# A two-layer hybrid transformer block on one core: first modulation pair loaded first, rotary turns moved to ScalarE, and three queues reordered

## The chip, the cores and the metric

The kernel runs on one core of a Trainium2 chip. The metric is the device time of the program in microseconds. TensorE does the matrix products, VectorE, ScalarE and GpSimd (POOL in the profile) the elementwise work, and SyncE (SP) issues all the transfers from HBM.

## The reference, cut to what matters

Two layers are applied to 256 tokens x and, beside them, 256 context tokens, all of width 1024 in float32. The second layer's context output is not needed.

```python
for l in range(DEPTH):                       # DEPTH = 2
    m  = silu(c) @ w_mod[l] + b_mod[l]       # six shifts, scales and gates for x
    mc = silu(c_ctx) @ w_mod[l] + b_mod[l]   # and for the context
    h, hc = rmsnorm(x)*g*(1+sc1)+sh1, rmsnorm(xc)*g*(1+csc1)+csh1
    a_b, a_c, a_u, q, k, v, r_g, r_u, d_v, d_g, gl = split(h @ w_in)
    y_b = window_attention(rotate(q), rotate(k), v, k_ctx, v_ctx, sink)
    ys = (short_conv(...) @ w_a_out, y_b @ w_b_out,
          (gelu(r_g) * rglru_bidir(...)) @ w_c_out,
          silu(layernorm(dwconv31(...))) @ w_d_out)
    x = x + gt1 * (sum(sigmoid(gl) * ys) @ w_out)
    x = x + gt2 * swiglu(rmsnorm(x)*g2*(1+sc2)+sh2)
out = rmsnorm(x) * g_final
```

In rotate, the 128 dimensions of a head are four blocks of 32: t becomes t*cos + (-t2, t1, -t4, t3)*sin. In the kernel the sign is part of the sine table, so that the turned operand is t with its blocks swapped in pairs.

## The kernel before

Activations are stored transposed: the 1024 features are eight rows (k = 0 to 7) of 128 partitions, the tokens are columns. W is 512 columns in layer 0 (tokens and context) and 256 in most stages of layer 1. Every float32 product is made from three products in a rounded format: the high part HH (or ZH) of the activation, its low part HL (ZL), and the high and low parts WH and WL of the weights. ScalarE makes a high half by a copy (`high`), POOL or VectorE makes the low half by a subtraction (`low`).

Weights come in slabs of 1 MB, two output tiles of 128 columns over all eight rows. There are two slots, s = 0 and 1, for RAW, WH and WL. A slab passes these steps: SP's load when both low halves of the slab before it in this slot are made, two high halves of 1024 columns on ScalarE, two low halves on POOL (in some stages of layer 1 the second on VectorE), 48 products on TensorE (line 474), then evacuation on ScalarE and VectorE. Slab n+2 is made ready by ScalarE and POOL while TensorE works at slab n+1. Two slabs are a pair; a stage is 4 to 8 slabs. The order of the work on each engine is written out by hand. Every engine works in its own order and waits for semaphores.

**Start.** SP loads x, then slab 0, then the eight modulation slabs of layer 0's first norm as four pairs (L383). TensorE sums squares, and then for each pair: 16 small products in 32 records (`mod_rows_of`, L579), a product that turns the rows to columns (`mod_columns`), and the products of the two rows of the pair before (`first_rows`). ScalarE copies the rows (`mod_copy`) and makes HH, VectorE makes MOD, AMP, S and HL.

**Keys and queries.** After the slabs of kv and q, ScalarE copies a tile to SBUF, TensorE multiplies it by the permutation ROT into bank 6 or 7 (`rotate`), and VectorE adds the cosine part and the turned sine part (`cosines`, `turned`). There is one such turn for the keys and one for each of the four query slabs, in each layer. With the last q slab come the first scores of attention, for head 0. The first d_in slab is cut up by the parts of head 0's attention; in layer 0 its scores of a third unit (the context's queries) come after 12 products and wait for query slab 2.

**a_out.** In the third pair of a_out (slabs 4 and 5) the layer norm of the conformer branch is finished: eight rows, for each one product with the norm's gain on VectorE, a sigmoid on ScalarE and a gate on VectorE. VectorE's `stage(..., some=(2, 3))`, which takes slabs 4 and 5 out of the banks, comes after it.

**Second norm.** After w_out, `norm_root` and `norm` prepare the rows of the feed-forward input. ScalarE's order is: roots and diagonals, `high` of slab 1 of ff_in0, a table load for the sigmoid, then the rows' HH (`norm_high`). POOL makes the low part of every second of the later rows (`norm_low`), behind both low halves of slab 1.

Of the kernel before, what the change touches and what calls it, by code (L numbers as in the profile page):

```python
# [22 lines left out]
DEPTH = 2  # L23
D = 1024
KC = D // P
# [115 lines left out]
def build(nc, stream, modw, lruw, xT, cT, prm, rope, consts, outT):  # L141
    with ExitStack() as ctx:
# [124 lines left out]
        def stage_sems(l):  # L267
# [39 lines left out]
            st("kv_a", "c0 v0 x0 x1")  # L307
            st("kv_v", "a0 a1 b0 s0 b1 s1")
            st("kv_p", "r0 r1")
            st("q_a", "c0 c1 x0 x1" if l == 0 else "c0 c1")  # L310
            st("q_v", "a0 b0 s0 b1 s1")
            st("q_p", "r0 r1")
# [53 lines left out]
        def _(sp):  # L366
# [63 lines left out]
        def _(pool):  # L430
# [27 lines left out]

            for first, end, halves in [r for r in runs if r[2]]:
                for l in range(DEPTH):  # L460
                    if first == pair_base(l, "ff_in0") + 1:
                        norm_low(l, "n2", seqs_of(l))
                    if l > 0 and first == pair_base(l, "kv") + 1:
                        norm_low(l, "n1", 2)
                with pool.Fori(first, end) as m:
                    for s in range(2):
                        for h in range(halves):
                            low(m, s, h)


        @block.tensor
        def _(pe):
# [201 lines left out]
            for p in range(MOD_FIRST // 2):  # L674
                pe.wait_ge(first_loaded[p], 32)
                for s in range(2):
                    mod_rows_of(s, MOD_HOMES[2 * p + s], p, s, 2)
                if p > 0:
                    pe.wait_ge(L[0]["mod_v"].sem, L[0]["mod_v"].at(0, f"m1_{p - 1}"))
                mod_columns(p, 2, PS[:, 4, 0:4 * MOD_FIRST].rearrange("p (h x) -> p h x", h=2)[:, :, 4 * p:4 * p + 4])  # L680
                if p > 0:
                    first_rows(2 * p - 2)
                    first_rows(2 * p - 1)
            first_rows(KC - 2)
            first_rows(KC - 1)
            for l in range(DEPTH):
# [26 lines left out]
                def rotate(st_a, st_p, n, s):  # L713
                    for t in range(2):
                        if f"c{t}" in st_a.names:
                            pe.wait_ge(st_a.sem, st_a.at(n, f"c{t}"))
                        else:
                            out_of(pe, l, "kv", 0)
                        mm(bank(6 + s, NX, t * NX), ROT, KR[t][:, 0:NX] if st_a is a["kv_a"] else QR[s][t], True, True).then_inc(st_p.sem, 1)


# [14 lines left out]
                pe.wait_ge(a["ci_a"].sem, a["ci_a"].at(KC - 1, "i1"))  # L736
                rotate(a["kv_a"], a["kv_p"], 0, 0)
# [35 lines left out]
                for n in range(1, 4):  # L773
# [1284 lines left out]
```

## Time and profile before

| | us |
|---|---|
| time, median of 3 runs | 2063.46 (2060.65 to 2063.71) |
| the profiled execution | 2059.77 |
| its span | 2058.0 |
| TensorE busy | 2025.8 (98%) |
| VectorE busy | 1110.7 (54%) |
| ScalarE busy | 880.6 (43%) |
| POOL busy | 820.2 (40%) |

The span goes from the first to the last instruction on the chip; what lies around it, 1.8 us here, is launch and end. Matmul records overlap, since their ends are modelled: the step from one start to the next is what a product costs. A float32 product without the three-part form has two records.

### The profile page before, as it was taken

The page shows a single profiled execution, that of the slowest core. Times are in us where ns is not written, and L with a number is a line of the kernel's source. Part 1 is how long each engine was busy: PE and PEld are TensorE (multiplying, and loading weights), DVE is VectorE, ACT ScalarE, POOL GpSimd, SP SyncE. Part 2 cuts the span into 40 slices and gives each one's busy share as a digit, 9 for nine tenths or more (in the row PEclk, how much of TensorE's full clock was granted, in tenths as well). Part 3 has the DMA queues.
Part 4 walks back from the last instruction along what each step waited for, and adds up shares of the span by engine and source line. Part 5 has one row for each costly group of instructions (what it writes and reads, how often), then busy time and mean ns, then how long its engine had stood idle before and what let it go on. Part 6 is the DMA issues. An engine that isn't in the chain of part 4 may idle for free.

```text
span 2058.0 us, 30588 instructions
## 1 busy us (share of the span) xinstructions
PE 2025.8 (98%) x11694; PEld 1695.7 (82%) x11694; DVE 1110.7 (54%) x2036; ACT 880.6 (43%) x1381; POOL 820.2 (40%) x355
## 2 busy tenths in 40 slices
PE   7999999999999999999999999999999999999998
PEld 4778788888888778777777788777899999999998
DVE  5895455567789741123111111479756888644555
ACT  4795444231222342224222212379765444545444
POOL 1003222343434444333334334410446887354443
PEclk9999999999999999999999999999999999999999
DMA  8222211222222223654534422422333555454553
GB/s 338 85 69 82 82 62 51 89 86 102 82 102 83 101 89 130 251 228 195 223 112 164 165 101 82 159 68 84 121 122 123 184 184 188 165 180 162 187 184 143
DMA packets 38705, 278.45 MB, mean 135 GB/s; under 512 B 4416, under 2 KB 4416, under 8 KB 5312
## 3 DMA queue, kind: packets, MB, share of 16 engines
q1 hardware_dynamic: 38592, 276.87, 37.1%
q8 instruction: 80, 1.31, 0.3%
q14 instruction: 33, 0.27, 0.0%
HBM read 275.80 MB, written 1.05 MB: 135 GB/s over the span
## 4 chain that ended last, share of the span: by engine, by line
PE 93%; DVE 2%; DMA 2%; ACT 2%; issue 1%; POOL 1%; SPq 0%; DVEq 0%; POOLq 0%; ACTq 0%
PE PS L474 90%; PE PS L579 2%; PE PS L756 1%; POOL WL L434 1%; DMA S<-in_modw 1%; ACT WH L852 1%; DMA RAW<-in_stream 1%; DMA CD<-in_lruw 0%; DVE PS L1301 0%; DVE CD L1304 0%; ACT TMP L852 0%; DVE LT L1304 0%; DVE HL L1304 0%; DVE WL L1301 0%; DVE X L1304 0%
## 5 line engine op out<-in xcount | busy, mean ns | idle before, releaser
L434 POOL TENSOR_TENSOR WL<-RAW,WH 128x1024 fp32r<-128x1024 f32 x336 | 808.9, 2426 | 1214.8 <-ACT WH L852 1214.8
L474 PE MATMUL PS<-HH,WH 128*128 128x512 f32 (+1 forms) x2272 | 800.0, 352 | 9.8 <-DVE HL L1304 4.9
L474 PE MATMUL PS<-HH,WL 128*128 128x512 f32 (+1 forms) x2272 | 778.9, 343 | 0.0
L474 PE MATMUL PS<-HL,WH 128*128 128x512 f32 (+1 forms) x2272 | 778.8, 343 | 0.0
L852 ACT ACTIVATE WH<-RAW 128x1024 fp32r<-128x1024 f32 x416 | 417.4, 1052 | 719.7 <-PE PS L474 666.1
L474 PEld LDWEIGHTS PS<-HH,WH 128*128 128x128 f32 x2272 | 429.3, 189 | 79.1 <-issue 22.5
L474 PEld LDWEIGHTS PS<-HL,WH 128*128 128x128 f32 x2272 | 429.7, 189 | 57.6 <-issue 5.5
L474 PEld LDWEIGHTS PS<-HH,WL 128*128 128x128 f32 x2272 | 429.0, 189 | 55.4
L474 PE MATMUL PS<-ZH,WH 128*128 128x512 f32 (+1 forms) x992 | 336.9, 340 | 2.8 <-POOL WL L434 1.7
L474 PE MATMUL PS<-ZH,WL 128*128 128x512 f32 (+1 forms) x992 | 335.6, 338 | 0.0
L474 PE MATMUL PS<-ZL,WH 128*128 128x512 f32 (+1 forms) x992 | 335.5, 338 | 0.0
L1304 DVE SCALAR_TENSOR_TENSOR PS<-G,PRM,PS 128x512 f32<-128x512 f32 (+1 forms) x464 | 254.3, 613 | 0.1
L474 PEld LDWEIGHTS PS<-ZH,WH 128*128 128x128 f32 x992 | 186.8, 188 | 29.0 <-issue 4.3
L474 PEld LDWEIGHTS PS<-ZH,WL 128*128 128x128 f32 x992 | 186.7, 188 | 22.7
L474 PEld LDWEIGHTS PS<-ZL,WH 128*128 128x128 f32 x992 | 186.8, 188 | 22.3
L1301 DVE TENSOR_TENSOR TMP<-TMP,PS 128x512 f32<-128x512 f32 (+1 forms) x56 | 31.6, 564 | 282.5 <-ACT TMP L852 267.9
L852 ACT ACTIVATE TMP<-PS 128x256 f32<-128x256 f32 (+1 forms) x173 | 84.2, 486 | 124.4 <-PE PS L756 52.1
L1301 DVE TENSOR_TENSOR PS<-TMP,PS 128x256 f32<-128x256 f32 (+1 forms) x84 | 46.2, 549 | 163.8 <-ACT TMP L852 149.5
L1301 DVE TENSOR_TENSOR WL<-RAW,WH 128x1024 fp32r<-128x1024 f32 x80 | 118.0, 1492 | 14.9 <-ACT WH L852 14.9
L1304 DVE SCALAR_TENSOR_TENSOR X<-PS,MOD,X 128x256 f32<-128x256 f32 (+1 forms) x96 | 41.3, 477 | 127.8 <-PE PS L474 127.7
L852 ACT ACT_TABLE_LOAD x50 | 64.2, 1283 | 1.6 <-PEq L2051 0.7
L474 PE MATMUL PS<-TMP,S 128*128 128x128 f32 (+2 forms) x288 | 61.4, 357 | 1.1 <-DVE CD L1301 1.1
(174 smaller groups left out, 1497.2 us busy)
## 6 DMA issues: line engine op xcount, KB each, us to landing
RAW<-in_stream SPq DMA_DIRECT2D x208, 1024.0 KB, 4.8
CD<-in_modw SPq DMA_DIRECT2D x42, 1024.0 KB, 7.1
CD<-in_lruw SPq DMA_DIRECT2D x2, 2048.0 KB, 8.3
X<-in_xT SPq DMA_DIRECT2D x2, 1024.0 KB, 8.1
S<-in_modw SPq DMA_DIRECT2D x2, 1024.0 KB, 14.0
G<-in_modw SPq DMA_DIRECT2D x2, 1024.0 KB, 22.0
RAW<-in_modw SPq DMA_DIRECT2D x1, 1024.0 KB, 17.0
TMP<-in_modw SPq DMA_DIRECT2D x1, 1024.0 KB, 18.8
```

The lines of the kernel that those rows point to most:

```text
L434: nc.gpsimd.tensor_tensor(WL[:, a:b], RAW[:, a:b], WH[:, a:b].bitcast(F32), ALU.subtract)\
L474: return nc.tensor.matmul(out, lhs, rhs, start=start, stop=stop)
L579: last = nc.tensor.matmul(PS[32 * g:32 * g + 32, 5 + q % 2, 0:2 * P], SILC[:, at:at + 32], w[:, k * 2 * P:(k + 1) * 2 * P], start=j == 0 a ...
L756: last = nc.tensor.transpose(bank(4 + u, P, q * P), PR[u % 2][:, q * P:(q + 1) * P], IDENT)
L852: return nc.scalar.activation(out, in_, f, **kw)
L1301: return V.tensor_tensor(out, x, y, op)
L1304: return V.scalar_tensor_tensor(out, x, sc, y, op0, op1)
```

## The change

It has five parts.

1. SP issues the first two modulation slabs ahead of weight slab 0, and the other six behind it. On TensorE, the pairs and the rows are woven: pair 0, columns 0, row 0, pair 1, row 1, columns 1, pair 2, row 2, columns 2, row 3, pair 3, row 4, columns 3, rows 5 to 7. ScalarE makes slab 0's high parts after the first `mod_copy`.
2. ROT's products are gone. ScalarE copies the four blocks of 32 partitions straight to their swapped places in bank 6 or 7, for both tiles at once, from the banks (queries) or from SBUF (keys). It waits until VectorE has read the bank's earlier contents. In layer 1, VectorE's cosines of a query tile wait for these copies. The first scores follow the last q slab.
3. In layer 1, slab 4 of a_out is gated and added before the layer-norm loop, its successor's first high half is made there too, the second high half after row 1, and the first of VectorE's low halves inside its loop.
4. ScalarE makes only the first high half of slab 1 of ff_in0 ahead of the second norm's rows, the second between or behind them, and loads the sigmoid table at the end.
5. POOL makes the low parts of those norm rows before the second low half of slab 1.

```diff
@@ sync
-            load(0, 0)
             for j, n in enumerate(MOD_ORDER):
+                if j == 2:
+                    load(0, 0)
@@ gpsimd
-                with pool.Fori(first, end) as m:
+                with pool.Fori(first, end - (end - 1 in ff_first)) as m:
...
+                if end - 1 in ff_first:
+                    l = ff_first.index(end - 1)
+                    for s, h in ((0, 0), (0, 1), (1, 0)):
+                        low(end - 1, s, h)
+                    norm_low(l, "n2", seqs_of(l))
+                    low(end - 1, 1, 1)
@@ tensor
+            first_mods(0)
+            first_columns(0)
+            first_rows(0)
+            first_mods(1)
+            first_rows(1)
+            first_columns(1)
+            first_mods(2)
+            first_rows(2)
+            first_columns(2)
+            first_rows(3)
+            first_mods(3)
+            first_rows(4)
+            first_columns(3)
+            for k in range(5, KC):
+                first_rows(k)
...
-                pe.wait_ge(a["ci_a"].sem, a["ci_a"].at(KC - 1, "i1"))
-                rotate(a["kv_a"], a["kv_p"], 0, 0)
...
-                    if n == 3:
-                        for u in range(2):
-                            scores(0, u, 0, 0)
-                        pe.wait_ge(a["q_v"].sem, a["q_v"].at(0, "s1"))
-                    rotate(a["q_a"], a["q_p"], n - 1, (n - 1) % 2)
-                pe.wait_ge(a["q_v"].sem, a["q_v"].at(1, "s1"))
-                rotate(a["q_a"], a["q_p"], 3, 1)
+                for u in range(2):
+                    scores(0, u, 0, 0)
@@ scalar
-            high(0, 0)
             for p in range(MOD_FIRST // 2):
                 mod_copy(p, p)
+                if p == 0:
+                    high(0, 0)
...
+                def swapped(source, s):
+                    for q in range(4):
+                        to, at = slice(32 * q, 32 * q + 32), slice(32 * (q ^ 1), 32 * (q ^ 1) + 32)
+                        last = fn(PS[to, 6 + s, 0:NT].rearrange("p (t n) -> p t n", t=2), source[at, :, 0:NX], ACT.Copy)
+                    return last
...
+                swapped(CD[:, 4 * NT:6 * NT].rearrange("p (t n) -> p t n", t=2), 0).then_inc(ks.sem, 1)
...
-                    for t in range(2):
-                        fn(QR[s][t], bank(2 * s + t, NX), ACT.Copy).then_inc(qs, 1)
+                    if n < 2:
+                        if s == 0:
+                            act.wait_ge(a["kv_v"].sem, a["kv_v"].at(0, "s1"))
+                    else:
+                        act.wait_ge(a["q_v"].sem, a["q_v"].at(n - 2, "s1"))
+                    swapped(PS[:, 2 * s:2 * s + 2, :], s).then_inc(qs, 1)
...
+                if l:
+                    tiles(b, 0)
+                    gate("ao")(4, 0, b)
+                    high(b + 1, 0, range(1))
...
+                    if l and k == 1:
+                        high(b + 1, 0, range(1, 2))
...
-                high(pair_base(l, "ff_in0"), 1)
+                high(pair_base(l, "ff_in0"), 1, range(1))
+                norm_high(l, "n2", 24, C, between=lambda: high(pair_base(l, "ff_in0"), 1, range(1, 2)))
                 table(ACT.Sigmoid)
-                norm_high(l, "n2", 24, C)
@@ vector
+                if l:
+                    dve.wait_ge(tile_done[0], 2 * (pair_base(l, "a_out") + 2) + 2)
+                    gated("ao")(4, 0, pair_base(l, "a_out") + 2)
...
+                    if l and k == 3:
+                        low(pair_base(l, "a_out") + 3, 0)
```

## Rows read from the trace of the kernel before

**Rows 1.** The page: busy time, share of the span, instructions.
```profile
PE 2025.8 (98%) x11694; PEld 1695.7 (82%) x11694; DVE 1110.7 (54%) x2036; ACT 880.6 (43%) x1381; POOL 820.2 (40%) x355
```
**Rows 2.** TensorE's waits: for whom, total us, times, longest.
```profile
PE PS L474 <- DVE HL L1304: 4.9, 5, 2.6
...
PE PS L474 <- DVE S L1301: 3.7, 1, 3.7
```
**Rows 3.** TensorE's timeline, start: start, us, what, count, idle before and its releaser.
```profile
19.36 3.57 PE L579 MATMUL PS<-S,SILC 128*32 128x256 f32 x32 [2.24 <-DMA S<-in_modw]
...
27.31 0.58 PE L474 MATMUL PS<-SELB,TMP 128*128 128x4 f32 x4 [1.12 <-ACT TMP L852]
...
46.31 0.50 PE L474 MATMUL PS<-HH,WH 128*128 128x512 f32 x1 [0.35 <-DMA CD<-in_lruw]
```
**Rows 4.** Timelines of VectorE, ScalarE and POOL, start.
```profile
17.87 3.35 DVE L1412 RECIPROCAL TMP<-TMP 128x512 f32<-128x512 f32 x1 [5.87 <-ACT TMP L852]
...
30.05 1.66 DVE L1304 SCALAR_TENSOR_TENSOR HL<-S,MOD,HH 128x256 fp32r<-128x256 f32 x4
...
42.51 1.99 ACT L852 ACTIVATE WH<-RAW 128x1024 fp32r<-128x1024 f32 x2
...
43.63 4.77 POOL L434 TENSOR_TENSOR WL<-RAW,WH 128x1024 fp32r<-128x1024 f32 x2 [20.08 <-ACT WH L852]
```
**Rows 5.** DMA issues of the first 60 us: count, KB each, median us to landing.
```profile
S<-in_modw SPq DMA_DIRECT2D x2, 1024.0 KB, 14.0
...
CD<-in_lruw SPq DMA_DIRECT2D x1, 2048.0 KB, 7.5
```
**Rows 6.** TensorE's timeline, layer 0, end of q and start of d_in.
```profile
222.75 1.88 PE L474 MATMUL PS<-TMP,S 128*128 128x512 f32 x4
224.46 1.89 PE L474 MATMUL PS<-S,CST 128*128 128x256 f32 x8
226.00 0.58 PE L474 MATMUL PS<-HH,WH 128*128 128x512 f32 x1
...
230.22 0.48 PE L474 MATMUL PS<-TMP,S 128*128 128x256 f32 x1 [1.07 <-DVE CD L1301]
```
**Rows 7.** Timelines of ScalarE, VectorE, POOL and TensorE, layer 1, kv and q.
```profile
1449.60 1.08 ACT L852 ACTIVATE CD<-PS 128x512 f32<-128x512 f32 x2 [0.73 <-PE PS L474]
...
1465.40 0.43 DVE L1301 TENSOR_TENSOR PS<-PS,ROPE 128x256 f32<-128x256 f32 x1 [0.64 <-PE PS L474]
...
1469.95 0.70 ACT L852 ACTIVATE TMP<-CD 128x256 f32<-128x256 f32 x2
...
1471.73 2.01 ACT L852 ACTIVATE WH<-RAW 128x1024 fp32r<-128x1024 f32 x2
...
1472.87 5.21 POOL L434 TENSOR_TENSOR WL<-RAW,WH 128x1024 fp32r<-128x1024 f32 x2 [1.40 <-ACT WH L852]
...
1479.03 0.42 ACT L852 ACTIVATE ZH<-TMP 128x256 fp32r<-128x256 f32 x1 [5.30 <-DVE TMP L1304]
...
1481.03 9.48 POOL L434 TENSOR_TENSOR WL<-RAW,WH 128x1024 fp32r<-128x1024 f32 x4 [2.94 <-ACT WH L852]
...
1493.48 0.47 PE L474 MATMUL PS<-HH,WH 128*128 128x256 f32 x1
```
**Rows 8.** Timelines of ScalarE and TensorE, layer 1, a_out.
```profile
1768.36 1.99 ACT L852 ACTIVATE WH<-RAW 128x1024 fp32r<-128x1024 f32 x2
...
1769.58 0.36 PE L474 MATMUL PS<-HH,WH 128*128 128x256 f32 x1 [3.74 <-DVE S L1301]
```
**Rows 9.** Timelines of TensorE and ScalarE at the second norms.
```profile
936.22 0.47 PE L474 MATMUL PS<-HH,WH 128*128 128x512 f32 x1 [1.54 <-DVE HL L1304]
...
1855.84 1.28 ACT L852 ACT_TABLE_LOAD   x1
...
1858.36 0.35 PE L474 MATMUL PS<-HH,WH 128*128 128x256 f32 x1 [2.60 <-DVE HL L1304]
```
**Rows 10.** Stretches: length, busy us of PE, PEld, DVE, ACT, POOL, then granted clock.
```profile
1770.00:1774.00 4.00, 4.00 (x23) 4.00 (x22) 3.71 (x4) 0.62 (x2) 2.81 (x1) 0.57 0.55 160
```

More of the change, by code:

```diff
@@ L672, in first_rows, with first_mods @@
                         last.then_inc(tile_done[0], 1)
-            for p in range(MOD_FIRST // 2):
+            def first_mods(p):
                 pe.wait_ge(first_loaded[p], 32)
@@ L711, in _ @@
                     gates(n - 1)
-                def rotate(st_a, st_p, n, s):
-                    for t in range(2):
[L715 to L719, printed above, removed]
                 b = pair_base(l, "kv")
@@ L852, in fn, with high @@
                 return nc.scalar.activation(out, in_, f, **kw)
-            def high(m, s):
+            def high(m, s, halves=range(2)):
                 act.wait_ge(raw_loaded[s], 16 * m + 16)
-                for h in range(2):
+                for h in halves:
                     x = slice(s * SLAB + h * HALF, s * SLAB + (h + 1) * HALF)
@@ L956, in diagonals, with norm_high @@
                     fn(tmp(1, c * P, (c + 1) * P), IDENT, ACT.Identity, scale=tmp(0, m + c, m + c + 1)).then_inc(inverse, 1)
-            def norm_high(l, nm, shift, c_all, some=None):
+            def norm_high(l, nm, shift, c_all, some=None, between=None):
                 na, nv = L[l][nm + "_a"].sem, L[l][nm + "_v"].sem
@@ L970, in norm_high @@
                         ins.then_inc(na, 1)
+                    if between is not None and k == (KC - 3 if c_all == 2 else KC - 1):
+                        between()
             def decay(l):
@@ L1230, in _ @@
                     fn(bank(5 + k % 2, W), row(CD, k, W), ACT.Sigmoid, bias=par(l, "ln_b", k)).then_inc(la.sem, 1)
-                    if k == KC // 2:
+                    if k == KC // 2 and l == 0:
                         tiles(b, 0)
                         high(b + 1, 0)
+                    if l and k == 1:
+                        high(b + 1, 0, range(1, 2))
                 table(ACT.Sigmoid)
-                gate("ao")(4, 0, b)
+                if l == 0:
+                    gate("ao")(4, 0, b)
                 tiles(b, 1)
@@ L1635, in _ @@
                     if n < 2:
-                        turned(a["q_v"], a["q_p"], n, n % 2, lambda t: query(n, t))
+                        turned(a["q_v"], a["q_a"], n, n % 2, lambda t: query(n, t))
                 dv, da = a["di_v"], a["di_a"]
@@ L1850, in _ @@
                         ln_gate(k - 1)
+                    if l and k == 3:
+                        low(pair_base(l, "a_out") + 3, 0)
                 ln_gate(KC - 1)
-                stage(l, "a_out", gated("ao"), some=(2, 3))
                 b = pair_base(l, "a_out") + 3
+                for s in range(l, 2):
+                    dve.wait_ge(tile_done[s], 2 * b)
+                    gated("ao")(4 + s, s, b - 1)
+                    if l:
+                        low(b, s)
                 dve.wait_ge(tile_done[0], 2 * b + 2)
```

31 lines of the change are left out of this document (11 added, 20 removed).

## The prediction

> **What bounds the kernel now.** I read the page first, then the waits of TensorE, then its timeline, and beside each of its gaps the timelines of the engine that ended the gap. The page says TensorE is busy 98% of a span of 2058.0 us [rows 1]. So only two things shorten the time: work taken off TensorE, and its gaps. The longest gaps stand in the waits [rows 2] and, one by one, in the timelines. Eight are longer than 0.9 us, and the change works at those of the modulation at the start [rows 3], of the first d_in slab of layer 0 [rows 6], the third a_out pair of layer 1 [rows 8], and the second norm of both layers [rows 9]. A gap can cost more than its length. After the 3.74 us gap at 1769.58 and the 2.60 us gap at 1858.36 the granted clock was at its lower level, 1.2 GHz, for a while (0.57 on the mean of 1770 to 1774) [rows 10]; after 1.07 us at 230.22 it stayed at 2.4 GHz. Counted in products, 24 of them took 4.44 us after the gap at 1769.58 and 2.85 us later: 1.6 us lost. I use 1.6 to 1.7 us for each such fall. The query slabs of layer 1 [rows 7] have no such gap yet. The Trainium skill (TensorE: Matmul & The Clock Gate, "What's actually happening") has the throttled state as the default and lets activity release it; by that rule a new gap is paid twice as well, and the trace agrees.
>
> **1. Rotary turns leave TensorE.** A call of rotate is two products, four records; two calls take 226.00 - 224.46 = 1.54 us [rows 6], 0.77 us a call. Five calls in each layer go. In their place ScalarE makes four copies of 32 partitions by 512. No row shows so few partitions. The nearest is the 128x512 copy: two in 1.08 us, a start every 0.50 [rows 7]. Below: if the price went by data moved, a quarter of that, 0.5 us for four; above: four that don't overlap at 0.60, 2.4 us. I take the whole price, 4 x 0.50 + 0.1 = 2.1 us, since the row's length goes with the columns. The Trainium skill (ScalarE: Activation LUTs, "What ACT_TABLE_LOAD costs") has one element a cycle in each lane, so that few partitions save nothing; by its figures four such copies are an estimated 2.1 us. No row here can show it.
>
> Layer 0, slabs of 11.3 us. The copies are hidden: the timelines have the weights of slab 2 ready at 195.1 and used at 199.2, and ScalarE's part comes 1.6 us later (without that slack of 4.1 us, 1.6 in each of two slabs). The turns of kv, q0 and q1 are saved: 3 x 0.77 = 2.3 us. Those of q2 and q3 are not. They stand between the scores (222.75) and the first d_in slab (226.00), which runs 12 products and then waits until 230.22 for VectorE [rows 6]. VectorE's chain begins with the scores, 7.5 us earlier, and its order is not changed. So the 1.54 us turn into a longer gap: 1.07 + 1.54 + about 0.2 = 2.8 us. It lies where the clock fell in the other rows (2.24, 2.60, 3.74) and above 1.54, where it did not: I count a fall at 7 in 10, +1.2. Term: -2.3 + 1.2 = **-1.1 us**.
>
> Layer 1, slabs of 5.7 us. Here the chain is short of time already: the last q slab waits 0.3 us in mid-slab for POOL (1485.85). ScalarE now copies kv's blocks after its last square roots: from 1469.95 [rows 7] to 1472.05. VectorE needs 1.7 us for its multiply and add (from 1465.40 [rows 7] to 1467.09 before, hidden then): 1473.8. The copy of q0 uses the same bank 6, so ScalarE waits for that, copies until 1475.9, and only then makes the high half of slab q2's weights, which is queued behind: 1475.85 where it was 1471.73 [rows 7], +4.1. POOL's first low half ends near 1475.5 before [rows 7], so 1479.6 after. TensorE would be there at 1477.27 - 2 x 0.77 = 1475.7: a gap of 3.9 us and a fall of the clock. Slab q2 ends at 1479.6 + 5.7 + 1.7 = 1487.0. Meanwhile VectorE takes q0's cosines 4.3 us later and with them its last two scans; ScalarE's ZH copy, which waits for these [rows 7], moves from 1479.03 to 1483.3. Behind it: copies of q1 until 1485.8, high half of slab q3 at 1485.7 (before 1479.88), POOL 1486.85 to 1489.25 and 1491.6 (two halves at 2.4) [rows 7]. Slab q3 starts at 1489.3 after a gap of 2.3 us, gets its second half at 1491.6, ends at 1495.9, or at 1496.9 with the clock down. With 1.7 us of scores d_in starts at 1497.6 or 1498.6; before 1493.48 [rows 7]. Term: +4.1 to +5.1, taken **+4.7 us**. With four copies at 0.5 us each chain link falls by 1.6: +0.5; at 2.4 us by 0.9: +5.6.
>
> **2. Start.** SP issues the first modulation pair ahead of the first weights. At some 420 GB/s a 1 MB slab lands every 2.5 us; the pair in S (14.0 us median from issue to landing) [rows 5] is there 2.5 us sooner, at 16.7 instead of 19.2. The weights land at 19.2, pair 2 at 24.2 as before. TensorE comes from the square sums at 17.0 with no gap and at the full clock, so pair 1 takes 1.9 us, as pairs 2 to 4 do, instead of 3.57 [rows 3], and ends near 19.0. That gains little: VectorE's reciprocal ends only at 17.87 + 3.35 = 21.22 [rows 4]. From there 0.5 for MOD and AMP, 1.7 for four S, 0.9 for the first two HL: row 0 at 24.3. ScalarE's weights (19.4 to 21.4) and POOL's low half (22.9) are in time. Then TensorE's order is rows 0, pair 2, row 1, columns 2, and so on. Rows 2 and 3 need columns + 2.74 + 0.85 = 3.6 us (27.31 to 30.05) [rows 3, 4], and the columns now stand behind a row. Without a low clock: row 0 to 25.7, pair 2 to 27.6, row 1 to 29.0, columns 29.0, row 2 at 32.6, columns 34.0, row 4 at 37.7, columns 39.1, rows 6 and 7 42.7 to 45.5. But between 19.0 and 24.3 TensorE has only the small column products, a gap in which I expect the clock to fall: +1.6 us ahead of the first columns, so last columns at 40.8. The next slab starts when ScalarE and POOL have made slab 1's weights, queued behind the last HH: HH ends 3.4 us after the columns, POOL's half 3.5 us after that (42.51 to 46.0) [rows 4]. So 47.7 against 46.31 [rows 3]; lruw lands 7.5 us after the last pair's products [rows 5], 47.1, and is not late. Ends: -0.3 (no fall) and +2.7. Term **+1.3 us**.
>
> **3. a_out, layer 1.** The gap of 3.74 us at 1769.58 is the wait for VectorE's gated sum of slab 4, which stands behind the whole layer-norm loop [rows 8]. Now gate and sum come ahead of it (done 1761.3), slab 6's first high half at 1760.4, its low half at 1764.0: slab 6 starts where slab 5 ends, 1765.6. That is 3.9 us earlier and no fall of the clock: 5.5 us. What is late next is slab 7. The loop starts 1.0 us later and now holds one low half of 1.2 us, ends at 1769.4; ScalarE's high half for slab 7 follows at 1769.0 (before 1768.36 [rows 8]), POOL's low half is done at 1772.7. TensorE is there at 1771.3: 1.4 us given back. Bounds -5.5 (slab 7 in time) and -2.5 (loop 1.6 us longer). Term **-4.2 us**.
>
> **4. Second norm.** ScalarE did two high halves (2.0) and a sigmoid table (1.3 + 0.2) ahead of the first HH [rows 9]; now one half. Layer 1: scaled rows are there at 1855.0, so HH 1855.05, HL 1855.5, first product 1856.1 instead of 1858.36 [rows 9]. Rows then come at VectorE's and POOL's pace: row 3 at 1859.05, row 7 at 1861.9, slab over at 1862.6 against 1865.7. The held-back half gives slab 1 its last low weights at 1864.5 where 1864.0 is wanted: 0.5. Term 3.1 - 0.5 = **-2.6 us** (bounds -3.5 and -1). Layer 0: four scaled rows end at 934.2, HL 935.1, so 1.0 us of the 1.54 at 936.22 [rows 9] goes; half 2 comes after row 5 and brings rows 6 and 7 back to their old times (POOL 944.1 and 945.4): **-0.7 us**.
>
> **Sum:** +1.3 - 1.1 + 4.7 - 4.2 - 2.6 - 0.7 = **-2.6 us**. Between these places TensorE runs without a gap, so that the terms add. The profiled execution took 2059.77 us (span 2058.0), so 2057.2 after; the median of the runs shown, 2063.46, is 3.7 us higher, and the forecast for the median is 2063.46 - 2.6 = **2060.9 us**. What counts as no change is 0.2%, 4.1 us, about what a measurement of this kernel can tell.
>
> **Rivals.** (a) The q chain of layer 1 holds: the copies cost by data, 0.5 us for four, or the wait for bank 6 costs little. Then that term is +0.5 and the sum -6.8: **2056.7**. For it: nothing but the small number of partitions. Against: every ScalarE row goes with its columns. (b) The other side: copies from PSUM to PSUM, of which no row shows any, take turns at reading and writing and cost double, 4.1 us for four. They are links of chains at three places. In layer 1 q0's and q1's copies stand one behind the other ahead of slab q3: 2 x 2.0 = +4.0. In both layers q3's copies stand ahead of the first exponential, which now leaves ScalarE idle until 2.5 us after the scores begin and would wait until 4.2: some +1.5 each. Sum -2.6 + 4.0 + 3.0 = +4.4: **2067.9**. For it: the copies read banks that VectorE's cosines read at the same time. Against: 256 columns cost 0.28 from PSUM to SBUF and no more where VectorE was reading too. It decides from where four cost 2.1 + 2.6/3.5 = 2.8 us: beyond that the kernel is slower than before. (c) The gaps close as planned and the clock never falls in the new ones: start -0.3, layer 0 -2.3, layer 1 +3.0, a_out -5.5, norms -4.0: -9.1, **2054.4**. For it: after 1.54 us at 936.22 the clock stayed up; against: two of the new gaps are well over 2 us.
>
> **Chances.** Forecast 0.60, of which 0.05 falls beyond 4.1 us on the fast side; (a) 0.18, (c) 0.10, (b) 0.12. So faster 0.33, same 0.55, slower 0.12. Range 2054.5 to 2066.0: it takes in (a), the bounds of the forecast's terms and half of what lies toward (b), and leaves out most of (c) and the far end of (b), under 2 in 10.
>
> **What would show it.** Start: first 512-column product near 24.3, second slab near 47.7. Layer 0: gap of 2.5 to 3 us before the third unit's scores. Layer 1: a new gap near 4 us before slab q2 that POOL ends, one near 2 us before q3, and four 32x512 copies at 0.5 us. a_out: no gap before slab 6, 1 to 2 us before slab 7. Second norm of layer 1: gap under 0.5 us and no low clock. Copies under 0.3 us each, or a q2 gap under 1 us, would make the prediction wrong.

## The result, and the profile after

| | before | after |
|---|---|---|
| median, 8 runs each, us | 2063.10 (2060.53 to 2063.71) | 2068.15 (2066.84 to 2069.74) |
| the profiled execution, us | 2059.77 | 2068.54 |
| its span, us | 2058.0 | 2066.8 |

The ratio is 1.0026, with an interval of 1.0018 to 1.0035: the kernel became slower by about 5.0 us. The forecast was 2060.9 us, 2.6 us faster than before, with a range of 2054.5 to 2066.0: both were wrong. The first fence shows the page of the profile after, the second its waits of TensorE (for whom, total us, times, longest); they answer to [rows 1, 2].

```profile
PE 2020.5 (98%) x11654; PEld 1690.7 (82%) x11654; DVE 1114.0 (54%) x2036; ACT 898.6 (43%) x1405; POOL 820.3 (40%) x355
```

```profile
PE PS L478 <- DVE HL L1328: 13.5, 7, 7.3
PE PS L478 <- POOL WL L433: 11.3, 9, 4.3
```

TensorE is busy 5.3 us less, with ten turns (40 records) gone, and its waits have grown by more. The wait for HL was 4.9 us with a longest of 2.6; it is now 13.5 us with one of 7.3. The wait for POOL's WL now holds one of 4.3 us. Both are in places where TensorE had none that long.

The timeline of TensorE after gives the places (start, us, what, count, idle before and its releaser):

```profile
17.54 1.94 PE L583 MATMUL PS<-S,SILC 128*32 128x256 f32 x32
...
27.90 0.80 PE L478 MATMUL PS<-HH,WH 128*128 128x512 f32 x1 [7.32 <-DVE HL L1328]
...
51.39 0.47 PE L478 MATMUL PS<-HH,WH 128*128 128x512 f32 x1 [0.17 <-issue]
...
232.71 0.80 PE L478 MATMUL PS<-TMP,S 128*128 128x256 f32 x1 [2.79 <-DVE CD L1325]
...
938.43 0.48 PE L478 MATMUL PS<-HH,WH 128*128 128x512 f32 x1 [1.33 <-DVE HL L1328]
...
960.58 0.64 PE L583 MATMUL PS<-CD,SILC 128*32 128x256 f32 x8 [1.38 <-DMA CD<-in_modw]
...
1484.12 0.36 PE L478 MATMUL PS<-HH,WH 128*128 128x256 f32 x1 [4.29 <-POOL WL L433]
...
1493.95 0.38 PE L478 MATMUL PS<-HH,WH 128*128 128x256 f32 x1 [1.95 <-POOL WL L433]
...
1511.45 0.38 PE L478 MATMUL PS<-TMP,S 128*128 128x128 f32 x1 [1.28 <-DVE CD L1325]
...
1785.34 0.39 PE L478 MATMUL PS<-ZH,WH 128*128 128x256 f32 x1 [1.25 <-POOL WL L433]
...
1864.74 0.36 PE L478 MATMUL PS<-HH,WH 128*128 128x256 f32 x1 [0.40 <-DVE HL L1328]
```

The 9984 products of the weight slabs come in the same order in both kernels. So the shift, the start of a product after less the start of the same product before, says where time is lost or won:

| stretch | shift at its end, us | change in it | predicted |
|---|---|---|---|
| start, to slab 1 | +5.1 | +5.1 | +1.3 |
| layer 0, q to the third unit's scores | +3.9 | -1.2 | -1.1 |
| layer 0, second norm and first modulation loads behind it | +4.2 | +0.3 | -0.7 |
| layer 1, up to the end of kv | +3.8 | -0.4 | 0 |
| layer 1, q and first d_in slab | +11.4 | +7.6 | +4.7 |
| layer 1, d_in to the middle of a_out | +12.6 | +1.2 | 0 |
| layer 1, third a_out pair | +8.6 | -4.0 | -4.2 |
| layer 1, second norm, to the end of slab 1 of ff_in0 | +6.2 | -2.4 | -2.6 |
| layer 1, the rest of the feed-forward, to the last product | +8.8 | +2.5 | 0 |

The profiled executions are 8.8 us apart and the medians 5.0. The two long stretches without an edit give +1.2 and +2.5 us. Most of that is a different rate of TensorE's products in the two executions, as the last section shows. Of the 2.5 us, 0.8 is a longer wait for POOL near the end (1.51 us where it was 0.63); over all kernels, those with nothing changed near it included, this wait was anywhere from 0.63 to 1.51 us. The -0.4 us of layer 1 up to kv is a fall of the clock ahead of layer 1's first norm, in the profile before and not in this one.

In layer 0's norm the shift falls by 1.7 us up to the slab at 938.43 and rises by 2.0 behind it, 1.38 of that at the wait at 960.58. The clock was low ahead of this slab in the profile before (0.57 from 931.00 to 934.60) and not in this one, but that isn't what brought the 1.7 us. rotary_only, which has the norm of before, ran here without a fall as well, and its slab started at the same place relative to the kernel before, behind a longer gap, 2.99 us for 1.54:

```profile
935.58 0.47 PE L472 MATMUL PS<-HH,WH 128*128 128x512 f32 x1 [2.99 <-DVE HL L1297]
```

**The start.** These are timelines of VectorE and POOL after, and then three groups by tile (count, ns shortest/median/longest, first and last start):

```profile
22.02 1.36 DVE L1328 SCALAR_TENSOR_TENSOR AMP<-MOD,PRM 128x2 f32<-128x2 f32 x2
23.41 3.64 DVE L1328 SCALAR_TENSOR_TENSOR S<-X,AMP,TMP 128x256 f32<-128x256 f32 x4
26.98 1.66 DVE L1328 SCALAR_TENSOR_TENSOR HL<-S,MOD,HH 128x256 fp32r<-128x256 f32 x4
...
20.95 4.64 POOL L433 TENSOR_TENSOR WL<-RAW,WH 128x1024 fp32r<-128x1024 f32 x2 [20.50 <-ACT WH L855]
```

```profile
L1328 DVE SCALAR_TENSOR_TENSOR AMP<-MOD,PRM x2: 147/720/1294, 22.0 to 23.2; 128x2 f32<-128x2 f32 x2
...
L1328 DVE SCALAR_TENSOR_TENSOR S<-X,AMP,TMP x4: 471/472/2456, 23.4 to 26.6; 128x256 f32<-128x256 f32 x4
...
L433 POOL TENSOR_TENSOR WL<-RAW,WH x2: 2335/2341/2347, 20.9 to 23.3; 128x1024 fp32r<-128x1024 f32 x2
```

Three of the four S take 0.47 us as before, and one, the first, takes 2.46: it begins at 23.41, inside POOL's second instruction, and ends at 25.87, just behind that instruction's end (23.3 + 2.3 = 25.6). The first AMP, of two columns, begins at 22.02 and takes 1.29 us, to the end of POOL's first (20.95 + 2.34 = 23.29). VectorE was stopped twice until a POOL instruction was over, and POOL lost nothing here (2.35 and 2.34 us). Before, POOL was done with these two halves when VectorE began: the S of the first two pairs took 476 to 483 ns each. The Trainium skill (SBUF — State Buffer, "SBUF: two separate sides") has this as a rule: VectorE with two operands in SBUF and GpSimd share a port pair, and whoever comes second is blocked for the whole instruction of the other. The traces agree, to within 0.3 us at both stops.

**The queries of layer 1.** Timelines of ScalarE, POOL and VectorE after:

```profile
1473.82 2.41 ACT L855 ACTIVATE PS<-CD 32x512 f32<-32x512 f32 x4
...
1478.07 2.29 ACT L855 ACTIVATE PS<-PS 32x512 f32<-32x512 f32 x4 [1.08 <-DVE TMP L1325]
1480.29 1.99 ACT L855 ACTIVATE WH<-RAW 128x1024 fp32r<-128x1024 f32 x2
...
1490.42 1.99 ACT L855 ACTIVATE WH<-RAW 128x1024 fp32r<-128x1024 f32 x2
...
1481.41 5.39 POOL L433 TENSOR_TENSOR WL<-RAW,WH 128x1024 fp32r<-128x1024 f32 x2 [6.18 <-ACT WH L855]
1491.54 9.38 POOL L433 TENSOR_TENSOR WL<-RAW,WH 128x1024 fp32r<-128x1024 f32 x4 [4.75 <-ACT WH L855]
...
1510.98 0.42 DVE L1325 TENSOR_TENSOR CD<-CD,PS 128x256 f32<-128x256 f32 x1
```

The chain can be followed as it was forecast: copies of the keys, VectorE's add, copies of query 0 into the same bank, and only then slab q2's high half (1480.29), POOL's low half, and TensorE's product at 1484.12. The same again for q3. ScalarE's copy of query 1 stands behind its last ZH copy, and that waited 5.49 us for VectorE's scans, until 1487.76. The last line is the end of query 3's turn at 1511.4, for which TensorE's first weighing by the scores ("o0", at 1511.45) now waits.

The granted clock beside these gaps, in stretches after (length, busy us of PE, PEld, DVE, ACT and POOL, then the clock, 1.00 for 2.4 GHz):

```profile
23.90:30.80 6.90, 2.90 (x10) 1.86 (x12) 4.74 (x8) 1.70 (x4) 1.69 (x1) 0.51 1.01 424
232.00:236.20 4.20, 3.49 (x9) 2.85 (x10) 4.03 (x12) 0.67 (x2) 3.85 (x2) 0.59 0.00 0
1484.00:1487.00 3.00, 2.40 (x13) 2.13 (x13) 2.96 (x4) 0.00 (x0) 2.80 (x2) 0.65 0.00 0
1494.00:1496.50 2.50, 2.12 (x13) 1.83 (x14) 0.76 (x2) 2.49 (x4) 2.50 (x2) 0.73 0.01 3
1764.00:1784.00 20.00, 20.00 (x168) 19.83 (x166) 15.84 (x30) 14.71 (x23) 8.30 (x4) 1.00 0.46 159
```

It fell in or after each of the gaps of 7.32, 2.79, 4.29 and 1.95 us. In the third a_out pair, where it was 0.57 after the gap that is gone [rows 10], it stays at 1.00.

### The profile page after: what moved, and what is told of

It reads as the page before. It is cut to its first block, busy times and chain, and to the rows that moved or that the text cites. A ratio compares the mean times of both kernels' runs of the same rounds, so it can differ in the third digit from the quotient of the medians.

```text
span 2066.8 us, 30512 instructions
## 1 busy us (share of the span) xinstructions
PE 2020.5 (98%) x11654; PEld 1690.7 (82%) x11654; DVE 1114.0 (54%) x2036; ACT 898.6 (43%) x1405; POOL 820.3 (40%) x355
## 3 DMA queue, kind: packets, MB, share of 16 engines
q8 instruction: 79, 1.29, 0.2%
## 4 chain that ended last, share of the span: by engine, by line
PE 92%; DVE 3%; ACT 2%; POOL 1%; issue 1%; DMA 1%; SPq 0%; DVEq 0%; POOLq 0%; ACTq 0%
PE PS L478 89%; PE PS L583 2%; POOL WL L433 1%; PE PS L764 1%; ACT WH L855 1%; DVE PS L1325 0%; DMA CD<-in_modw 0%; DVE S L1328 0%; ACT PS L855 0%; DMA RAW<-in_stream 0%; DVE LT L1328 0%; ACT TMP L855 0%; DVE HL L1328 0%; DVE CD L1325 0%; DMA PRM<-in_prm 0%
## 5 line engine op out<-in xcount | busy, mean ns | idle before, releaser
L478 PE MATMUL PS<-HH,WH 128*128 128x512 f32 (+1 forms) x2272 | 801.5, 353 | 22.3 <-DVE HL L1328 13.5
L1325 DVE TENSOR_TENSOR WL<-RAW,WH 128x1024 fp32r<-128x1024 f32 x80 | 118.0, 1491 | 18.4 <-ACT WH L855 18.4
## 6 DMA issues: line engine op xcount, KB each, us to landing
S<-in_modw SPq DMA_DIRECT2D x2, 1024.0 KB, 12.3
TMP<-in_modw SPq DMA_DIRECT2D x1, 1024.0 KB, 18.4
```

Of the source, the lines that this page charges most:

```text
L478: return nc.tensor.matmul(out, lhs, rhs, start=start, stop=stop)
L1325: return V.tensor_tensor(out, x, y, op)
```

## The experiments

Every kernel was timed in five rounds against the kernel before. "Alone" means the kernel before with this part of the change and no other.

### The parts alone

**start_only**: part 1 alone.

```diff
             for j, n in enumerate(MOD_ORDER):
+                if j == 2:
+                    load(0, 0)
...
+            first_mods(0)   # and the woven order, as in the change
...
                 mod_copy(p, p)
+                if p == 0:
+                    high(0, 0)
```

> The kernel before with part 1 alone (DMA order, woven start, later first high halves). Theory read from the two traces: the first weights' low halves on POOL now run beside VectorE's first AMP and S, which take 1.36 and 3.64 us there instead of 0.23 and 1.67, and the clock falls in the long gap behind; the second slab starts 5.1 us later and the whole kernel is 5 us slower. Rival, the prediction's term: +1.3 us, the rest of the measured 5 us belonging to the other parts.

Measured: 2067.95 against 2062.43 us, ratio 1.0024 (1.0016 to 1.0033); slab 1 starts 5.5 us later. Its timelines of VectorE and TensorE repeat the picture, one S stopped and the gap of 7.32:

```profile
23.86 3.64 DVE L1321 SCALAR_TENSOR_TENSOR S<-X,AMP,TMP 128x256 f32<-128x256 f32 x4
...
28.34 0.80 PE L475 MATMUL PS<-HH,WH 128*128 128x512 f32 x1 [7.32 <-DVE HL L1321]
...
51.80 0.47 PE L475 MATMUL PS<-HH,WH 128*128 128x512 f32 x1 [0.16 <-issue]
```

So the start costs as much as the whole change.

**rotary_only**: part 2 alone.

```diff
-                    rotate(a["q_a"], a["q_p"], n - 1, (n - 1) % 2)
...
-                        fn(QR[s][t], bank(2 * s + t, NX), ACT.Copy).then_inc(qs, 1)
+                    swapped(PS[:, 2 * s:2 * s + 2, :], s).then_inc(qs, 1)
```

> The kernel before with part 2 alone (no ROT products, ScalarE swaps the blocks). Theory from the traces: layer 0 -1.2 us, layer 1 +7.5 us (gaps near 4.3 before slab q2, 2.0 before q3, and 1.3 before the first weighing of values, which waits for query slab 3), so +6.3 us. Rival, the prediction's term: layer 0 -1.1, layer 1 +4.7, so +3.6 us, without the gap before the first weighing.

Measured: 2068.73 us, ratio 1.0033 (1.0021 to 1.0046). The shift falls by 1.0 us over layer 0's queries and grows by 6.6 over layer 1's, with the gaps of the whole change, 4.29 us before slab q2, 1.64 before q3, and the unforeseen one:

```profile
1505.44 1.16 PE L472 MATMUL PS<-TMP,S 128*128 128x128 f32 x8 [1.23 <-DVE CD L1294]
```

**aout_only**: part 3 alone.

```diff
+                if l:
+                    tiles(b, 0)
+                    gate("ao")(4, 0, b)
+                    high(b + 1, 0, range(1))
...
+                    if l and k == 3:
+                        low(pair_base(l, "a_out") + 3, 0)
```

> The kernel before with part 3 alone (layer 1, slab 4 of a_out gated before the layer-norm loop). Prediction's term -4.2 us, trace of the change -4.0 us: both say 4 us faster, gap of 1.3 us before slab 7 and none before slab 6. Rival: the gap only moves with the phase in which the stage is entered, and the part alone gives less than 2 us.

Measured: 2057.26 us, ratio 0.9978 (0.9969 to 0.9986), 5.2 us faster. The shift falls by 3.9 us at slab 6 and by 1.6 more over it, since the clock stays up, and rises by 1.4 ahead of slab 7, at a wait of 1.25: 4.1 us in all.

**norm2_only**: parts 4 and 5 alone, in both layers.

```diff
-                high(pair_base(l, "ff_in0"), 1)
+                high(pair_base(l, "ff_in0"), 1, range(1))
+                norm_high(l, "n2", 24, C, between=lambda: high(pair_base(l, "ff_in0"), 1, range(1, 2)))
                 table(ACT.Sigmoid)
-                norm_high(l, "n2", 24, C)
...
+                    for s, h in ((0, 0), (0, 1), (1, 0)):
+                        low(end - 1, s, h)
+                    norm_low(l, "n2", seqs_of(l))
+                    low(end - 1, 1, 1)
```

> The kernel before with parts 4 and 5 alone (second norm). Theory from the traces: layer 1 -2.8 us, layer 0 -1.4 us at the norm and +1.7 us back at a modulation slab that now lands late, because POOL's last low half, which frees RAW slot 1, comes 10 us later and SP's queue waits for it: -2.5 us in all, with a DMA gap near 958. Rival, the prediction's term: -3.3 us and no such gap.

Measured: 2061.21 us, ratio 0.9993 (0.9985 to 1.0002), no difference that can be told. By place there are two: layer 1 gains 2.8 us and gives back 0.4 at slab 1 of ff_in0, and layer 0 gains 0.9 at its slab 0 and gives back 2.2 soon after. The fence shows TensorE and SP's queue in this kernel, the next SP's queue in the kernel before:

```profile
934.95 0.47 PE L479 MATMUL PS<-HH,WH 128*128 128x512 f32 x1 [0.27 <-DVE HL L1311]
955.10 1.07 PE L584 MATMUL PS<-CD,SILC 128*32 128x256 f32 x16 [0.61 <-DMA CD<-in_modw]
957.55 1.07 PE L584 MATMUL PS<-CD,SILC 128*32 128x256 f32 x16 [1.38 <-DMA CD<-in_modw]
...
947.36 0.33 SPq L368 DMA_DIRECT2D RAW<-in_stream  x1
948.02 1.19 SPq L371 DMA_DIRECT2D CD<-in_modw  x2
```

```profile
937.32 0.33 SPq L368 DMA_DIRECT2D RAW<-in_stream  x1
...
949.00 1.19 SPq L371 DMA_DIRECT2D CD<-in_modw  x2
```

The second low half of slab 1 now comes behind POOL's norm rows. SP may load the next slab into this slot only when that half is made: at 947.36, where it was 937.32. The modulation weights, queued right behind it, were issued a little sooner than before and land later, since 1 MB goes ahead of them.

The medians of the four parts add to +5.5 + 6.3 - 5.2 - 1.2 = +5.4 us, against +5.0 for all of them. Each median is known to about 2 us only, so this alone shows no more than that nothing large is shared. By place the parts agree with the whole change to within 0.4 us at slab 1 (+5.5 and +5.1), in layer 0's queries (-1.0 and -1.2) and in a_out (-4.1 and -4.0), and to 1.0 in layer 1's queries (+6.6 and +7.6) and in layer 0's norm (+1.2 and +0.3).

### What in the start costs

**start_load**: the order of the transfers and of ScalarE's high parts from part 1, TensorE's order as before. Against start_only:

```diff
-            first_mods(0)   # and the rest of the woven order
+            for p in range(MOD_FIRST // 2):
+                first_mods(p)
+                first_columns(p)
+                if p > 0:
+                    first_rows(2 * p - 2)
+                    first_rows(2 * p - 1)
+            first_rows(KC - 2)
+            first_rows(KC - 1)
```

> Part 1 without the weave: the first modulation pair is loaded first and slab 0's high parts are made after the first row copy, but TensorE keeps its old order (pair, columns, then the two rows of the pair before). Theory (two causes): POOL's low halves still run beside VectorE's first AMP and S, so these take 1.4 and 3.6 us and the first HL starts near 27.0; yet pair 2 is not queued behind row 0 and starts at 24.2, its columns near 28.1 (27.31 before), and the kernel ends +0.8 us. Rival (the collision alone explains the start's +5.5): +4 us or more.

Measured: 2061.90 against 2062.57 us, ratio 1.0003 (0.9992 to 1.0014); slab 1 at +0.2. The same S is stopped, and nobody waits for it:

```profile
23.07 3.66 DVE L1314 SCALAR_TENSOR_TENSOR S<-X,AMP,TMP 128x256 f32<-128x256 f32 x4
...
23.34 1.93 PE L580 MATMUL PS<-RAW,SILC 128*32 128x256 f32 x16 [3.09 <-DMA TMP<-in_modw]
27.70 0.58 PE L475 MATMUL PS<-SELB,TMP 128*128 128x4 f32 x4 [0.98 <-ACT TMP L861]
```

Pair 1 of the modulation (the second) runs at 23.34 while VectorE is stopped, and its columns come at 27.70, near the 27.31 of before [rows 3]. So the stop alone doesn't cost the 5.5 us; it costs where TensorE stands behind row 0.

**start_woven**: only TensorE's woven order; transfers and ScalarE as before. Against start_only:

```diff
-                if j == 2:
-                    load(0, 0)
...
-                if p == 0:
-                    high(0, 0)
```

> Part 1 with the weave alone: TensorE's new order of pairs, columns and rows, but slab 0 loaded first and its high parts made first, as before. Theory: no collision (S in 1.67 us), but pair 2 stands behind row 0, which is ready at 27.1, and all later columns behind a row each: the second columns start near 31.8 instead of 27.3, the second slab near 49; +2.8 us. Rival (the collision alone): within 1 us of the kernel before.

Measured: 2065.98 us, ratio 1.0011 (1.0001 to 1.0021); slab 1 at +4.6, more than the +2.8 expected, though the four S take 1.67 us:

```profile
27.40 0.80 PE L474 MATMUL PS<-HH,WH 128*128 128x512 f32 x1 [3.16 <-DVE HL L1319]
...
50.87 0.47 PE L474 MATMUL PS<-HH,WH 128*128 128x512 f32 x1 [0.16 <-issue]
```

**start_pool_waits**: start_only, and POOL's first low half waits until VectorE has made the first four S.

```diff
+            pool.wait_ge(L[0]["n1_v"].sem, 5)
             for s in range(2):
                 for h in range(2):
                     low(0, s, h)
```

> As start_only, but POOL begins slab 0's low halves only when VectorE's first four S are made. Theory (VectorE's two-operand ops in SBUF run at half speed beside POOL's subtraction, whatever they compute): AMP and S go back to 0.23 and 1.67 us, and now the four HL, beside POOL, take 3.6 us instead of 1.66; row 0 can start near 26.2 instead of 28.3 and the kernel ends 1.5 to 2 us sooner than start_only, at +3.5 us. Rival (AMP and S are slow for another cause, such as X or the bank being read elsewhere): S stays at 3.6 us and HL at 1.66.

Measured: 2066.11 against 2062.49 us, ratio 1.0017 (1.0008 to 1.0026), 1.9 us better than start_only. The stop moves with POOL to the next instructions. By tile and in TensorE's timeline:

```profile
L1322 DVE SCALAR_TENSOR_TENSOR S<-X,AMP,TMP x4: 480/480/486, 22.1 to 23.3; 128x256 f32<-128x256 f32 x4
...
L1322 DVE SCALAR_TENSOR_TENSOR HL<-S,MOD,HH x4: 473/1524/2585, 23.7 to 29.1; 128x256 fp32r<-128x256 f32 x4
...
L435 POOL TENSOR_TENSOR WL<-RAW,WH x2: 2519/2532/2545, 23.8 to 26.3; 128x1024 fp32r<-128x1024 f32 x2
```

```profile
26.68 0.80 PE L476 MATMUL PS<-HH,WH 128*128 128x512 f32 x1 [6.31 <-DVE HL L1322]
...
50.22 0.47 PE L476 MATMUL PS<-HH,WH 128*128 128x512 f32 x1 [0.17 <-issue]
```

Every S is at 0.48 us, and two of the four HL take about 2.6, one for each of POOL's instructions. That the stop is POOL's doing is shown by this: only POOL was moved. It is no half speed, as I had expected (3.6 us for four): an instruction waits for the end of POOL's, and the four took from 23.7 to 29.5. And the four woven kernels give one law. From the first row's product to slab 1 they take 51.39 - 27.90 = 23.5, 51.80 - 28.34 = 23.5, 50.87 - 27.40 = 23.5 and 50.22 - 26.68 = 23.5 us. In the ten kernels with the order of before, these are 18.4 to 20.0 us, with row 0 at 27.6 to 28.6.

### What in the rotary part costs

**rotary_early**: part 2 alone, and VectorE finishes query 2 ahead of its first maxima of the scores, not behind.

```diff
-                    if n < 2:
-                        turned(a["q_v"], a["q_a"], n, n % 2, lambda t: query(n, t))
+                    turned(a["q_v"], a["q_a"], n, n % 2, lambda t: query(n, t))
...
-                turned(a["q_v"], a["q_a"], 2, 0, lambda t: query(2, t))
```

> Part 2 alone, and VectorE turns query slab 2 before the first maxima instead of behind both normalisations. Theory (the last turns' 1.5 us were given back at waits for VectorE's late turns of slabs 2 and 3): the gap of 2.8 us before the third unit's scores in layer 0 and the 1.2 us before the first weighing in layer 1 go, the rest stays: -4.5 us in layer 0 at the end of the first d_in slab, +4.5 in layer 1 for its slabs q2 and q3; in all near 0 instead of rotary_only's +6.3. Rival (the gaps come from ScalarE's later exponentials behind four copies): the gaps stay within 0.5 us, total +6.

Measured: 2063.58 us, ratio 1.0006 (0.9997 to 1.0015), 5.3 us better than rotary_only, each against its own before. By place it is -5.6 us in layer 0, where -4.5 was expected, and +5.1 in layer 1. The gaps before the third unit's scores (2.79) and before the first weighing (1.23) are gone; the gaps before slabs q2 and q3 stay at 4.29 and 1.65.

**rotary_weights_first**: rotary_early, and in layer 1 ScalarE makes the high halves of slabs q2 and q3 ahead of the swaps and of the last ZH copy.

```diff
                     tiles(b + n // 2, n % 2)
+                    if l and n < 2:
+                        high(b + n // 2 + 1, n % 2)
+                    if l and n == 1:
+                        z_high(KC - 1)
                     q_in(n, n % 2, b + n // 2)
-                    if n < 3:
+                    if n == 2 or l == 0 and n < 2:
                         high(b + n // 2 + 1, n % 2)
-                    if n == 0:
+                    if l == 0 and n == 0:
                         z_high(KC - 1)
```

> As rotary_early, and in layer 1 ScalarE makes the weights' high halves of slabs q2 and q3 ahead of the block copies of q0 and q1 (and of the wait for the last ZH). Theory (the weights are late since they queue behind the copies, the wait for bank 6 and the ZH): the gaps of 4.3 and 1.6 us before q2 and q3 shrink to about 1.2 and 0, no low clock there; -6 us against rotary_early, -5 to -7 against the kernel before. Rival (the slabs wait for the banks' evacuation, which now comes later behind the high halves): gaps of 2 us or more remain and less than 2 us are won.

Measured: 2063.17 us, ratio 1.0004 (0.9995 to 1.0014). Here the theory that the weights' lateness is the cost failed and its rival held:

```profile
1474.86 0.36 PE L472 MATMUL PS<-HH,WH 128*128 128x256 f32 x1 [2.42 <-DVE CD L1298]
1485.65 0.36 PE L472 MATMUL PS<-HH,WH 128*128 128x256 f32 x1 [3.37 <-DVE CD L1298]
```

The gaps are now ended by VectorE's cosines: a query's bank is freed by them, and they wait for the swap. The swap of q0 now stands behind the high halves (it ran from 1471.56 to 1473.85), and the swap of q1 behind the last ZH copy (1482.35 to 1484.64). Layer 1's queries still cost 4.8 us. The swap is a link of two chains there, and taking it out of one leaves it in the other.

**rotary_layer0**: ScalarE's swap and the early turn in layer 0 only; layer 1 turns on TensorE as before. Against rotary_early:

```diff
+                if l:
+                    rotate(a["kv_a"], a["kv_p"], 0, 0)
...
+                    if l:
+                        for t in range(2):
+                            fn(QR[s][t], bank(2 * s + t, NX), ACT.Copy).then_inc(qs, 1)
+                        return
```

> Part 2 in layer 0 alone, with VectorE's early turn of query slab 2; layer 1 keeps its ROT products. Theory (five calls at 0.77 us and the old 1.1 us gap before the third unit's scores go, and 11 us slabs hide ScalarE's copies): -5.0 to -5.5 us. Rival (something behind layer 0's attention gives it back, as the slabs' POOL and DMA work does in layer 1): under 3 us.

Measured: 2059.11 us, ratio 0.9984 (0.9975 to 0.9993), 3.4 us faster, where 5.0 to 5.5 were expected. By place TensorE is 5.7 us ahead at the end of layer 0's first d_in slab and loses some of that in stretches without an edit, where its rate differs; the median alone can't tell 3.4 from 5.

### Toward a better kernel

**norm2_layer1**: parts 4 and 5 in layer 1 only. Against norm2_only:

```diff
+                    if l == 0:
+                        low(end - 1, 1, 1)
                     norm_low(l, "n2", seqs_of(l))
-                    low(end - 1, 1, 1)
+                    if l > 0:
+                        low(end - 1, 1, 1)
...
+                if l == 0:
+                    high(pair_base(l, "ff_in0"), 1)
+                    table(ACT.Sigmoid)
+                    norm_high(l, "n2", 24, C)
```

> Parts 4 and 5 in layer 1 alone; layer 0 as before. Theory (layer 0's part gives its gain back at the late modulation slab): no DMA gap near 958, layer 1 -2.8 us, total -2.8 us against norm2_only's -1.2. Rival (layer 0's part is neutral): total -1.2 to -1.5 us.

Measured: 2058.78 us, ratio 0.9982 (0.9973 to 0.9991), 3.7 us faster; no wait for the modulation weights in layer 0.

**best**: aout_only, norm2_layer1 and rotary_layer0 in one kernel, with the start of before; the diff is these three's.

> Part 3, parts 4 and 5 in layer 1 alone, part 2 in layer 0 alone with the early turn; the start as before. If the parts add: -5.2 - 2.8 - 5.3 = -13.3 us. Rival (they share slack): -9 us or less.

Measured: 2049.53 (2048.89 to 2050.47) against 2062.49 us, ratio 0.9936 (0.9923 to 0.9950). It beats both kernels; the three parts by themselves had gained 5.2 + 3.7 + 3.4 = 12.3 us, together 13.0. Its longest waits of TensorE for POOL's WL and VectorE's HL are 1.2 and 1.8 us, where they were 4.3 and 7.3 after the change. The page's line:

```profile
PE 2020.0 (99%) x11674; PEld 1691.4 (83%) x11674; DVE 1113.9 (54%) x2036; ACT 890.4 (43%) x1393; POOL 821.1 (40%) x355
```

## Why the prediction was wrong

**Start, predicted +1.3, measured +5.1. The step that failed: "From there 0.5 for MOD and AMP, 1.7 for four S, 0.9 for the first two HL: row 0 at 24.3."** The durations were taken from a stretch in which POOL was silent [rows 4], while the same paragraph had POOL's low half running until 22.9. In fact POOL ran from 20.95 to 25.59 and stopped VectorE twice, 1.29 - 0.15 and 2.46 - 0.47, 3.1 us together; 0.5 more came since the reciprocal itself began later (18.36 for 17.87 [rows 4]), and row 0 came at 27.90. The rest of the step was right: pair 0 at 17.54 without a gap at 1.94 us, a clock that fell while TensorE waited, and from row 0 to slab 1 47.7 - 24.3 = 23.4 us, where the runs had 23.5 four times. Without any stop, the chain from 21.7 would give a row 0 at 24.8 and a slab 1 at 48.3, 2.0 us late, near the forecast; no run had such a start. What the prediction did not draw from its own sum is that by this law row 0 would have to come at 46.3 - 23.5 = 22.8 for the weave to break even, which is 1.1 us after VectorE's reciprocal ends in the kernel after (21.7). Its chain from there to row 0 is 3.1 us without any stop, so the weave could not win here. Its order puts the second pair behind row 0, so that TensorE idles through VectorE's chain instead of working in it.

The price of a stop could have been read in the kernel before. It has some fifty, and one stands in the very stretch of [rows 7]: of these two instructions in layer 1's queries, with both operands in SBUF, the second began at 1472.94 beside POOL's subtraction and took 2.91 us instead of 0.69.

```profile
L1301 DVE TENSOR_TENSOR PS<-TMP,CD x2: 689/1797/2905, 1472.3 to 1472.9; 128x512 f32<-128x512 f32 x2
```

**Rotary, layer 1, predicted +4.7, measured +7.6 (+6.6 by itself).** The chain was the one predicted, and its sizes were short. Four copies took 2.41 us from SBUF and 2.29 between banks, not 2.1: 594 and 564 ns for one, and with no overlap, near the end that I had called upper, for which the prediction had +5.6. With the shift at the end of kv taken off, slab q2 starts at 1480.4 (1479.6 forecast) and d_in at 1499.3 (1497.6 or 1498.6): +5.8 us, so that the copies' size makes about 1.1 of the miss. **The step that failed for the other 1.8 is that the turns of q2 and q3 were counted as saved.** The clock fell in both gaps; I had left the second open. Taking the turns out brings a wait that the prediction had not named: with the turns gone, the scores and the start of d_in come sooner relative to VectorE's turn of query 3, and the first weighing waits 1.28 us for it. This is the step of layer 0, "So the 1.54 us turn into a longer gap", and it holds in layer 1 as well. rotary_early shows it: with VectorE's order mended the wait goes in both layers. The stop of the paragraph above is a link of the same chain: the last ZH copy waits for the scans behind that instruction, and the swap of q1 for the copy. It is there in all these kernels (2.84 us at 1481.73 in the kernel after). No run took it out, so what it costs stays open.

**Rotary, layer 0, predicted -1.1, measured -1.2.** Right in each part: a gap of 2.79 us (2.8 forecast), the clock down after it (0.59), the copies hidden.

**a_out, predicted -4.2, measured -4.0.** Right: no gap before slab 6, 1.25 us before slab 7 (1.4 forecast), no low clock.

**Second norm, layer 1, predicted -2.6, measured -2.4.** Right: a gap of 0.40, -2.9 us in all, and 0.5 given back on slab 1, where TensorE waits for POOL.

**Second norm, layer 0, predicted -0.7, measured +0.3 (+1.2 by itself).** The gain came (0.9 by itself, 1.4 by the end of the slab in the whole change), and more than that was given back at a place that I had not followed: a POOL instruction that is moved behind others frees its slot later, and SP, which loads in order, sends that slab right ahead of the modulation weights that TensorE wants next. The step that failed is the last of its term, that the second half only "brings rows 6 and 7 back to their old times": I followed POOL's queue to the slab's own products and not to SP.

**Rivals.** None was what happened. (b), slow copies between banks, came nearest in time (2067.9) and was wrong: those copies are the faster of the two kinds, so that its nearness to 2068.15 is luck. (a) and (c) needed the query chain or the clock to hold; neither did. The sum's misses are +3.8 at the start, +2.9 in layer 1's queries and +1.0 in layer 0's norm, all to one side. But for 1.1 us of copies, each is a wait or a stop left out, and none of the range's ends held one. Two readings of the trace before were off without weight: it has nine gaps over 0.9 us after the first 15 us, not eight, and POOL's first low half for slab q2 ended at 1475.29, not 1475.5, since the two of the row took 2.42 and 2.84 us and not the same.

## What to carry to other kernels

When an edit moves work of VectorE or of POOL, lay their two timelines over each other and charge VectorE with the rest of POOL's instruction wherever it meets one; a duration from a stretch where the other is silent doesn't hold. Work put first on the engine that waits is worth something only if the chain it waits for is no longer than what it gave up doing in between: write the end as "first result plus the rest" and ask how early the first result would have to be. And a step moved down in one queue is to be followed into the queue that it releases, loads above all; where several edits come in one change, the sum of their separate prices is what to ask for, since some of them (here three, one of them with its order mended, together 13 us) may be worth keeping.

## What the runs showed of the hardware that was not expected

- An instruction of VectorE with two operands in SBUF, met by POOL's 128x1024 subtraction, ends only behind POOL's, the later the more columns it has: 0.01 to 0.04 us with up to 16 columns, 0.28 to 0.29 with 256, 0.55 to 0.56 with 512, 1.08 to 1.09 with 1024, in the traces of all fourteen kernels, where 49 to 53 instructions each were stopped by more than 0.2 us. None of them read a tensor in PSUM. Where VectorE was first, POOL waited: its subtraction at 663.98 in the kernel before took 3.54 us instead of 2.4, beside two such instructions of VectorE that ran from 663.96 to 665.24. At the start this cost up to 2.1 us on an instruction of 0.47 and 1.1 on one of two columns.
- Copies of 32 partitions on ScalarE to other partitions of a bank take 594 ns each, as those of 128 partitions by 512 do [rows 7], and follow one another without the overlap that these have: four in 2.41 us, a start every 0.60, against 0.50. From one bank to another they take 564 ns each, four in 2.29 us.
- TensorE's rate differs between executions at a granted clock of 1.00. In the feed-forward of layer 1, the same 1000 products of 256 columns took 117.3 us in the profile before and 118.7 in the one after, 2.82 and 2.85 us for 24. In another stretch, of 500 products from slab 7 of layer 1's a_out on, before and after took 59.3, aout_only 58.7 and norm2_layer1 60.0. Differences of this size over stretches as long as the two without an edit make most of their 1.2 and 2.5 us, and a single pair of profiles 8.8 us apart can so have medians 5.0 apart.
- The clock doesn't go by the length of a gap alone. In and behind rotary_only's gap of 2.99 us it stayed at 1.00 (932.6 to 939.0), while it fell at gaps of 1.95 and 2.79 in the kernel after. In the kernel before it was 0.57 from 931.00 to 934.60, where TensorE made small products ahead of layer 0's second norm; in the one after it was 1.00 there, and those products took 1.5 us less. The slab behind them waits for VectorE, and gained nothing by it in rotary_only.
- In kernels with the start of before, slab 1 began anywhere from 46.0 to 48.4 us.
